# The normed operand of two stages made tile by tile in the last units of the stage in front, without a barrier at these two borders

## The chip, the cores and the metric

The kernel runs on one core of a Trainium2 chip. A core has a matrix engine (TensorE, "PE" in the profile, with its weight loads as "PEld"), a vector engine (VectorE, "DVE"), a scalar engine (ScalarE, "ACT"), GpSimd ("POOL") and a queue engine (SyncE, "SP"). Each runs its own instruction stream, and they wait for each other by semaphores. The metric is device time in microseconds (us) of the whole kernel, the median of several runs.

## What is computed

One step of a decoder layer on 1024 prompt tokens and 8 sample tokens (1032 columns in all), model width 1024, all in fp32:

```
x = x + 0.5 * swiglu(rmsnorm(x, g_ffn1), ffn1_gate, ffn1_up, ffn1_down)   # FFN 1
h = rmsnorm(x, g_mix);  proj = h @ w_in                                   # projections
...  # RWKV-7 branch y_a and S5 branch y_b from proj
merged = gates[..., :D_MODEL] * (y_a @ w_a_up) + gates[..., D_MODEL:] * (y_b @ w_b_up)
x = x + merged @ w_out                                                    # merge, out product
x = x + 0.5 * swiglu(rmsnorm(x, g_ffn2), ffn2_gate, ffn2_up, ffn2_down)   # FFN 2
# rmsnorm(x, g) = x * rsqrt(mean(x * x, axis=-1) + 1e-6) * g
```

## The kernel before

Activations lie transposed in SBUF: 128 channels on the partitions, 8 tiles (`DT`) of 1032 tokens. A **unit** is one 128-column stripe of a weight matrix times all tokens. The PE instructions of a unit are in `product`: for each of `kt` tiles of the contraction three groups of three matmuls of 344 columns (the fp32 operands are split into a high and a low part, high x high, high x low, low x high). So a unit with kt = 8 is 24 groups, and one of FFN 1's last down-projection units, with kt = 5, is 15. Two sets of three PSUM banks alternate between units.

Around each unit four things move. SP loads the weight stripe (`load_units`, L164) into one of two slots `wraw`; POOL splits it into `whi` (L176) and `wlo` (L179) as soon as the unit that used the slot two before is done; PE multiplies; DVE empties the banks and frees the set (`set_free`). The engines' order is that in which the code is written, engine by engine.

The norm is applied late. The operand of a normed product is x times g (`hhi` by ACT at L313, `hlo` by DVE at L321, a high and a low part), without the row factor; squares of x (ACT, L254) are summed over the 8 tiles (DVE, L261 and L264) into `ssum`, PE turns these into sums over channels (L274) inside the second unit of the stage, DVE takes the inverse root, PE spreads it to all partitions (L285), DVE copies it to `rstd` (L305), and whoever empties a bank multiplies by it. The first two units thus need only `hhi` and `hlo`; the third needs a free bank set and so `rstd`.

Each stage is a function that emits one program per engine. FFN 1 stands in a block of its own; projections and S5 stage share a block; the merge (products with `w_a`, then eight units with `w_out`, the out product) and FFN 2 have a block each. At the end of a block all engines meet at a barrier. So in front of the projections and of FFN 2 the order is: last unit on PE, last add of the product into x on DVE (L435, L2520), barrier, then ACT and DVE make `hhi` and `hlo` tile by tile from x (`h_act`, `h_dve`) and PE starts on the first tile (`h_products`). In the projections ACT first issues the DMA that saves x to DRAM (L812), and SP loads two constants (L785, L786) and the weights of the third and fourth unit; the weights of the first two are loaded and split ahead, in the stage in front (`Ahead`).

Of the kernel before, what the change touches and what calls it, by code (L numbers as in the profile page):

```python
# [12 lines left out]
P = 128  # L13
# [232 lines left out]

def squares_act(act, g, n, ready=None):

    for k in range(DT):
        if ready:  # L250
            ready(k)
        if k >= 2:
            act.wait_ge(g.ssum_step, DT * n + k - 1)
        act.activation(g.tmp[:, k % 2, :], g.x[:, k, :], ACT.Square).then_inc(g.sq_ready, 1)  # L254

def square_sum(v, g, n, k):

    v.wait_ge(g.sq_ready, DT * n + k + 1)
    if k == 0:  # L260
        v.tensor_copy(g.ssum[:, :], g.tmp[:, 0, :]).then_inc(g.ssum_step, 1)  # L261
    else:
        v.wait_ge(g.ssum_step, DT * n + k)
        v.tensor_tensor(g.ssum[:, :], g.ssum[:, :], g.tmp[:, k % 2, :], ALU.add)\  # L264
            .then_inc(g.ssum_step, 1)

def sums_pe(pe, g, n):

    pe.wait_ge(g.ssum_step, DT * (n + 1))  # L270
    if n:
        pe.wait_ge(g.rstd_ready, 3 * n)
    for j in range(NSS):
        last = pe.matmul(g.ps[0:SS, 6, j:j + 1], g.ssum[:, j * SS:(j + 1) * SS], g.seg[:, 2:3],  # L274
                         start=True, stop=True)
    last.then_inc(g.norm_ss, 1)
# [30 lines left out]

def h_act(act, g, gcol, n, ready=None):

    for k in range(DT):  # L310
        if ready:
            ready(k)
        act.activation(g.hhi[:, k, :], g.x[:, k, :], ACT.Copy, scale=g.vec[:, gcol + k:gcol + k + 1])\  # L313
           .then_inc(g.hhi_ready, 1)

def h_dve(v, g, gcol, n):

# [8 lines left out]
def h_products(pe, g, n, u, use, first_two, rest):  # L327
# [4 lines left out]
    if first_two:  # L332
        product(pe, g, 0, 0, u, DT, 0, use[0], 0, hi, lo, h_wait)
        product(pe, g, 0, 0, u + 1, DT, 1, use[1], 0, hi, lo, None, (6, lambda: sums_pe(pe, g, n)))
# [10 lines left out]
def ffn_block(nc, g, w_up, w_down, gcol, before=None, after=None, setup=None, ahead=None, loaded=False):  # L345
# [20 lines left out]
    with nc.Block() as block:  # L366
# [29 lines left out]
        def _(v):  # L396
            st = Steps(v, g.dve_s, g.dve_n)
            h_dve(v, g, gcol, n0)
# [5 lines left out]
            for size, k0, u, a, use, use1 in groups():  # L404
# [23 lines left out]
                if after and k0 + size == FT:  # L428
                    after["down"](v, ud)
                    continue  # L430
                with v.Fori(0, DT // 2) as i:
# [9 lines left out]
            g.dve_end = st.n  # L441

        @block.scalar
        def _(act):
            if before:
                before["scalar"](act)
            h_act(act, g, gcol, n0, before and before["x_ready"](act))
            squares_act(act, g, n0)
# [11 lines left out]
            if after:  # L460
                after["scalar"](act)
            if setup:
# [3 lines left out]
        def _(pe):  # L466
# [5 lines left out]
            for size, k0, u, a, use, use1 in groups():  # L472
                h_products(pe, g, n0, u, (use, use1), k0 == 0, size - (k0 == 0))
# [11 lines left out]
    g.a_tiles, g.norms, g.dve_n = a0 + FT, n0 + 1, g.dve_end  # L485
# [285 lines left out]
def proj_block(nc, g, w_in, shift, f_dram, x_dram, last_out, gp_dram, d_in, u_dram, us_dram, ahead, block):  # L771
# [10 lines left out]
    if block:  # L782
        @block.sync
        def _(sp):
            sp.dma_start(g.shift[:, :, :], shift).then_inc(g.sh_in, 16)  # L785
# [25 lines left out]
        def _(act):  # L811
            act.dma_start(x_dram, g.x[:, :, :]).then_inc(g.x_out, 16)  # L812
            h_act(act, g, V_GMIX, n0)
            squares_act(act, g, n0)
# [28 lines left out]
        def _(v):  # L843
            st = Steps(v, g.dve_s, g.dve_n)
            h_dve(v, g, V_GMIX, n0)
# [1594 lines left out]
def plan_merge(nc, g):  # L2440
    o = g.x_end
# [3 lines left out]
    g.mt, o = g.at("merge_t", o, [P, 2, TOK])  # L2445
    assert o <= g.u_off, (o, g.u_off)
    S = nc.alloc_semaphore
# [5 lines left out]
def merge_block(nc, g, w_a, w_out, gate_dram, wb_dram, x_dram, ahead):  # L2453
# [5 lines left out]
    t = g.mt  # L2459
# [4 lines left out]
    with nc.Block() as block:  # L2464
# [20 lines left out]
        def _(act):  # L2485
            for k in range(WT):
                act.activation(g.yahi[:, k, :], g.ya[:, k, :], ACT.Copy).then_inc(g.ya_hi_s, 1)
            for n in range(DT):
                act.wait_ge(g.m_ready, n + 1)
                act.activation(g.hhi[:, n, :], t[:, n % 2, :], ACT.Copy).then_inc(g.m_hi, 1)  # L2490
# [3 lines left out]
            for k in range(DT // 2, DT):  # L2494
                act.dma_start(g.x[:, k, :], x_dram[:, k, :]).then_inc(g.x_in[k], 16)

        @block.vector
        def _(v):
# [4 lines left out]
            for n in range(DT):  # L2503
# [11 lines left out]
                v.tensor_tensor(g.hlo[:, n, :], t[:, j, :], g.hhi[:, n, :].bitcast(F32),  # L2515
                                ALU.subtract).then_inc(g.m_split, 1)
            for n in range(DT):
                v.wait_ge(g.x_in[n], 32)
                v.wait_ge(g.unit_done, uo + n + 1 + WSLOTS)
                v.scalar_tensor_tensor(blocks(g.x[:, n, :]), acc(g, n % 2), 0.5, blocks(g.x[:, n, :]),  # L2520
                                       ALU.mult, ALU.add).then_inc(g.set_free[n % 2], 1)

        @block.tensor
        def _(pe):
# [3 lines left out]
            with pe.Fori(0, DT // 2) as i:  # L2528
                for j in range(2):
                    product(pe, g, i, 2, uo + j, DT, j, use_o[j], 1, part(g.hhi), part(g.hlo),  # L2530
# [7 lines left out]
def build(nc, a, o):  # L2538
# [36 lines left out]
    ffn_block(nc, g, a["ffn1_up"], a["ffn1_down"], V_G1,  # L2575
              before={"sync": first_loads, "scalar": first_x,
                      "x_ready": lambda act: lambda k: act.wait_ge(g.x_in[k], 16)},
              setup=s5_setup(g, s5_dram), ahead=ahead(a["w_mix"], DT, RT))
    consts, f_load = rwkv_early(g, f_dram, a["tabs"], a["lora_up"], a["g_up"], a["rw_sel"])
    with nc.Block() as block:  # L2580
        proj_block(nc, g, a["w_mix"], a["shift"], f_dram, x_dram, o["last"], s5_dram["in"], a["s5_d"], u_dram, us_dram,
# [5 lines left out]
    merge_block(nc, g, a["w_a"], a["w_out"], gate_dram, wb_dram, x_dram, ahead(a["ffn2_up"], DT))  # L2587

    n1 = g.norms + 1  # L2590
    ends = [n + 1 + FT + len(FFN_GROUPS) * DT // 2 for n in g.uses]
# [37 lines left out]
    ffn_block(nc, g, a["ffn2_up"], a["ffn2_down"], V_G2, loaded=True,  # L2629
# [108 lines left out]
```

## Time and profile before

| | us |
|---|---|
| median of 3 runs | 2828.43 (2824.94 to 2828.95) |
| profiled execution | 2827.97 |
| its span, first to last instruction | 2826.2 |
| PE busy | 2631.1 (93%) |
| DVE busy | 1143.4 (40%) |
| POOL busy | 891.9 (32%) |
| ACT busy | 429.9 (15%) |

Busy time is a sum over the span; it does not say who waits for whom. Matmuls are pipelined: a group of three is shown with a length of some 0.63 us, but the next one starts 0.47 us after it, so the pace is read from starts.
### The profile page before, as it was taken

The page shows a single profiled execution, that of the slowest core. Times are in us where ns is not written, and L with a number is a line of the kernel's source. Part 1 is how long each engine was busy: PE and PEld are TensorE (multiplying, and loading weights), DVE is VectorE, ACT ScalarE, POOL GpSimd, SP SyncE. Part 2 cuts the span into 40 slices and gives each one's busy share as a digit, 9 for nine tenths or more (in the row PEclk, how much of TensorE's full clock was granted, in tenths as well). Part 3 has the DMA queues.
Part 4 walks back from the last instruction along what each step waited for, and adds up shares of the span by engine and source line. Part 5 has one row for each costly group of instructions (what it writes and reads, how often), then busy time and mean ns, then how long its engine had stood idle before and what let it go on. Part 6 is the DMA issues. An engine that isn't in the chain of part 4 may idle for free. (4 is left out here: it accounts for less than half of the span.)

```text
span 2826.2 us, 47930 instructions
## 1 busy us (share of the span) xinstructions
PE 2631.1 (93%) x20824; PEld 2558.5 (91%) x20824; DVE 1143.4 (40%) x1637; ACT 429.9 (15%) x764; POOL 891.9 (32%) x445
## 2 busy tenths in 40 slices
PE   7999999999989989997899999569899999999997
PEld 7999999999989989996788887459899999999997
DVE  5743834713154555334444544253242122122224
ACT  3000100000020001122344443110111000000011
POOL 3444434444333432234100000005334444443432
PEclk9999999999999999998999989679999999999998
DMA  3112121111144242233310000024111111111111
GB/s 119 47 47 60 65 62 60 61 51 50 47 158 102 90 161 83 75 132 104 96 28 16 16 14 3 18 87 175 45 38 39 58 45 37 52 48 41 52 38 74
DMA packets 79684, 183.23 MB, mean 65 GB/s; under 512 B 11504, under 2 KB 34672, under 8 KB 78784
## 3 DMA queue, kind: packets, MB, share of 16 engines
q1 hardware_dynamic: 55456, 133.71, 15.4%
q10 hardware_dynamic: 24096, 47.59, 5.1%
q8 instruction: 103, 1.69, 0.3%
q14 instruction: 29, 0.24, 0.0%
HBM read 139.65 MB, written 40.44 MB: 64 GB/s over the span
## 5 line engine op out<-in xcount | busy, mean ns | idle before, releaser
L176 POOL TENSOR_TENSOR whi<-wraw,small 128x1024 fp32r<-128x1024 f32 (+3 forms) x214 | 363.3, 1697 | 1868.2 <-PE ps L210 1809.5
L210 PE MATMUL ps<-hhi,whi 128*128 128x344 f32 x3120 | 673.6, 325 | 54.5 <-POOL wlo L179 33.0
L210 PE MATMUL ps<-hlo,whi 128*128 128x344 f32 x3120 | 668.3, 323 | 0.0
L210 PE MATMUL ps<-hhi,wlo 128*128 128x344 f32 x3120 | 665.1, 322 | 0.0
L210 PEld LDWEIGHTS ps<-hhi,whi 128*128 128x128 f32 x3120 | 531.6, 191 | 57.3 <-issue 36.9
L210 PEld LDWEIGHTS ps<-hlo,whi 128*128 128x128 f32 x3120 | 534.3, 191 | 0.0
L210 PEld LDWEIGHTS ps<-hhi,wlo 128*128 128x128 f32 x3120 | 526.2, 190 | 0.0
L179 POOL TENSOR_TENSOR wlo<-wraw,whi 128x1024 fp32r<-128x1024 f32 (+3 forms) x214 | 516.0, 2411 | 16.8
L210 PE MATMUL ps<-ahi,whi 128*128 128x344 f32 x1056 | 223.8, 320 | 0.0
L210 PE MATMUL ps<-alo,whi 128*128 128x344 f32 x1056 | 223.5, 320 | 0.0
L210 PE MATMUL ps<-ahi,wlo 128*128 128x344 f32 x1056 | 223.0, 319 | 0.0
L435 DVE SCALAR_TENSOR_TENSOR x<-ps,x 128x1032 f32 x56 | 69.0, 1233 | 345.8 <-PE ps L210 345.8
L455 ACT ACTIVATE tmp<-tmp 128x1032 f32<-128x1032 f32 x44 | 47.0, 1068 | 888.1 <-DVE tmp L408 888.1
L411 DVE TENSOR_TENSOR tmp<-ps,rstd 128x1032 f32<-128x1032 f32 x44 | 54.2, 1232 | 304.5 <-PE ps L210 304.5
L210 PEld LDWEIGHTS ps<-ahi,whi 128*128 128x128 f32 x1056 | 177.0, 188 | 0.0
L210 PEld LDWEIGHTS ps<-alo,whi 128*128 128x128 f32 x1056 | 176.9, 188 | 0.0
L210 PEld LDWEIGHTS ps<-ahi,wlo 128*128 128x128 f32 x1056 | 176.8, 188 | 0.0
L408 DVE TENSOR_TENSOR tmp<-ps,rstd 128x1032 f32<-128x1032 f32 x44 | 54.2, 1233 | 178.0 <-PE ps L210 177.3
L419 DVE TENSOR_TENSOR alo<-tmp,ahi 128x1032 fp32r<-128x1032 f32 (+1 forms) x44 | 85.9, 1951 | 54.6 <-ACT ahi L457 54.6
L457 ACT ACTIVATE ahi<-tmp 128x1032 fp32r<-128x1032 f32 (+1 forms) x44 | 47.0, 1068 | 387.9 <-DVE tmp L416 387.9
L2048 PE MATMUL ps<-rw_x,rw_t 64*64 64x64 f32 x1280 | 86.5, 233 | 7.1 <-DVEq L1392 6.0
L2051 PE MATMUL ps<-rw_t,rw_x 64*64 64x64 f32 x1280 | 84.5, 230 | 0.0
(401 smaller groups left out, 2552.4 us busy)
## 6 DMA issues: line engine op xcount, KB each, us to landing
wraw<-ffn_up SPq DMA_DIRECT2D x88, 512.0 KB, 3.6
wraw<-ffn_down SPq DMA_DIRECT2D x32, 384.0 KB, 3.2
wraw<-ffn_down SPq DMA_DIRECT2D x32, 320.0 KB, 2.9
wraw<-w_mix SPq DMA_DIRECT2D x18, 512.0 KB, 3.6
gates<-gate_out ACTq DMA_DIRECT2D x16, 516.0 KB, 2.7
wraw<-w_gates SPq DMA_DIRECT2D x16, 512.0 KB, 3.7
f_mixed<-fmix ACTq DMA_DIRECT2D x14, 516.0 KB, 3.7
rw_f<-f_mixed SPq DMA_DIRECT2D x8, 896.0 KB, 5.7
```

What stands on the lines that cost most here:

```text
L176: pool.tensor_tensor(g.whi[:, s, 0:n], g.wraw[:, s, 0:n], g.zero.to_broadcast([P, n]), ALU.add).then_inc(g.w_hi, 1)
L179: pool.tensor_tensor(g.wlo[:, s, 0:n], g.wraw[:, s, 0:n], g.whi[:, s, 0:n].bitcast(F32), ALU.subtract).then_inc(g.w_split, 1)
L210: last = pe.matmul(g.ps[:, 3 * bank_set + b, 0:BLK], w[:, s, k * P:(k + 1) * P], x(k, b), start=(k == 0 and first), stop=(k == kt - 1 and ...
L408: v.tensor_tensor(blocks(g.tmp[:, 0, :]), acc(g, 0), blocks(g.rstd[:, :]), ALU.mult)\
L411: v.tensor_tensor(blocks(g.tmp[:, 1, :]), acc(g, 1), blocks(g.rstd[:, :]), ALU.mult)\
L419: v.tensor_tensor(g.alo[:, bass.ds(i, 1), :], g.tmp[:, 1:2, :], g.ahi[:, bass.ds(i, 1), :].bitcast(F32), ALU.subtract).then_inc(g.a_ready, 1)
L435: v.scalar_tensor_tensor(xt, acc(g, j), 0.5, xt, ALU.mult, ALU.add)\
L455: act.activation(g.tmp[:, 0, :], g.tmp[:, 0, :], ACT.Silu).then_inc(g.silu_done, 1)
L457: act.activation(g.ahi[:, bass.ds(i, 1), :], g.tmp[:, 1:2, :], ACT.Copy).then_inc(g.a_hi, 1)
L2048: pe.matmul(g.ps[r, 6 + n, p * N:(p + 1) * N], T[r, n, 1, p, :], g.X[r, j - 1, n, p, :], start=True, stop=True)
L2051: last = pe.matmul(g.ps[r, 6 + n, (4 + p) * N:(5 + p) * N], g.X[r, j - 1, n, p, :], T[r, n, 1, p, :], start=True, stop=True)
```

## The change

Three things. (1) FFN 1, projections and S5 stage now share one block, and merge and FFN 2 another: no barrier at these two borders. (2) The operand of the next normed stage is made in the last eight units of the stage in front: once DVE has added unit k into x, ACT makes `hhi` and the square of tile k, and DVE makes `hlo` and adds the square of tile k - 1 behind the add of unit k. Only the last tile's work comes behind the last add. (3) As `hhi` and `hlo` are now written while the out product still runs, the merge keeps its merged operand in tiles of its own (`mhi`, `mlo`, where FFN's `ahi` and `alo` lie), its inputs move into the space of `hhi` and `hlo`, and the squares and sums of the second border get tiles of their own (`tmp2`, `ssum2`). What the barrier had ordered for SP at the first border is now waited for by name.

```
+def h_hi(act, g, gcol, k):
+    act.activation(g.hhi[:, k, :], g.x[:, k, :], ACT.Copy, scale=g.vec[:, gcol + k:gcol + k + 1])\
+       .then_inc(g.hhi_ready, 1)
+def h_lo(v, g, gcol, n, k):
+    v.wait_ge(g.hhi_ready, DT * n + k + 1)
+    v.scalar_tensor_tensor(g.hlo[:, k, :], g.x[:, k, :], g.vec[:, gcol + k:gcol + k + 1],
+                           g.hhi[:, k, :].bitcast(F32), ALU.mult, ALU.subtract).then_inc(g.h_ready, 1)
...
 def ffn_block(...)
-    with nc.Block() as block:
+    if block:
...
         def _(v):
-            h_dve(v, g, gcol, n0)
+            if not normed:
+                h_dve(v, g, gcol, n0)
...
+                if gnext is not None and k0 + size == FT:
+                    for k in range(DT + 1):
+                        if k < DT:
+                            v.wait_ge(g.unit_done, ud + k + 1 + WSLOTS)
+                            v.scalar_tensor_tensor(blocks(g.x[:, k, :]), acc(g, k % 2), 0.5, blocks(g.x[:, k, :]),
+                                                   ALU.mult, ALU.add).then_inc(g.set_free[k % 2], 1)
+                        if k:
+                            h_lo(v, g, gnext, n0 + 1, k - 1)
+                            square_sum(v, g, n0 + 1, k - 1)
...
         def _(act):
+            if gnext is not None:
+                downs = [n + FT + (len(FFN_GROUPS) - 1) * DT // 2 for n in s0]
+                for k in range(DT):
+                    act.wait_ge(g.set_free[k % 2], downs[k % 2] + k // 2 + 2)
+                    h_hi(act, g, gnext, k)
+                    square_act(act, g, n0 + 1, k, g.tmp)
...
 def proj_block(...)
         def _(sp):
+            sp.wait_ge(g.unit_done, u0 + WSLOTS)
+            sp.wait_ge(g.su_ready, 12)
+            for n in range(3):
+                sp.wait_ge(g.su_out[n], 16 * 4)
             sp.dma_start(g.shift[:, :, :], shift).then_inc(g.sh_in, 16)
...
         def _(act):
             act.dma_start(x_dram, g.x[:, :, :]).then_inc(g.x_out, 16)
-            h_act(act, g, V_GMIX, n0)
-            squares_act(act, g, n0)
...
         def _(v):
-            h_dve(v, g, V_GMIX, n0)
...
 def merge_block(...)
         def _(act):
+            for k in range(DT):
+                act.wait_ge(g.set_free[k % 2], use_o[k % 2] + k // 2 + 2)
+                h_hi(act, g, V_G2, k)
+                square_act(act, g, n1, k, g.tmp2)
         def _(v):
-            for n in range(DT):
...
+            for n in range(DT + 1):
+                if n < DT:
+                    v.wait_ge(g.x_in[n], 32)
+                    v.wait_ge(g.unit_done, uo + n + 1 + WSLOTS)
+                    v.scalar_tensor_tensor(blocks(g.x[:, n, :]), acc(g, n % 2), 0.5, blocks(g.x[:, n, :]),
+                                           ALU.mult, ALU.add).then_inc(g.set_free[n % 2], 1)
+                if n:
+                    h_lo(v, g, V_G2, n1, n - 1)
+                    square_sum(v, g, n1, n - 1, g.ssum2, g.tmp2)
```

The order of ACT's program at the first border, before (from FFN 1's last turn, L457, to the save of u, L817):

```order
L457 ACTIVATE ahi<-tmp 128x1032 [waits a_full]
L366 UNCONDITIONAL_BRANCH [waits s5_part_out2,s5_part_out1,s5_part_out0]
L810 UNCONDITIONAL_BRANCH [waits barrier_Pool_Activation_PE_DVE_SP_release]
L812 DMA x_mid<-x 128x8256
L313 ACTIVATE hhi<-x,vec 128x1032 x8
L254 ACTIVATE tmp<-x 128x1032 x2
L254 ACTIVATE tmp<-x 128x1032 [waits square_sums] x6
L817 DMA u<-u_turned 128x1024 [waits u_ready]
```

and now (L314 is the old L313, L251 the old L254, L849 the old L812; the last three of the eight pairs stand here):

```order
L314 ACTIVATE hhi<-x,vec 128x1032 [waits set_free1]
L251 ACTIVATE tmp<-x 128x1032 [waits square_sums]
L314 ACTIVATE hhi<-x,vec 128x1032 [waits set_free0]
L251 ACTIVATE tmp<-x 128x1032 [waits square_sums]
L314 ACTIVATE hhi<-x,vec 128x1032 [waits set_free1]
L251 ACTIVATE tmp<-x 128x1032 [waits square_sums]
L847 UNCONDITIONAL_BRANCH [waits s5_part_out2,s5_part_out1,s5_part_out0]
L849 DMA x_mid<-x 128x8256
L852 DMA u<-u_turned 128x1024 [waits u_ready]
```

The sixteen instructions have moved in front of the stage's border, one pair behind each add into x, and the save of x has moved behind them.

On DVE at the second border, before (from the add of the out product's seventh unit into x to the first step of the inverse root):

```order
L2520 SCALAR_TENSOR_TENSOR x<-ps,x 128x1032 [waits unit_done,x_in6]
L2520 SCALAR_TENSOR_TENSOR x<-ps,x 128x1032 [waits unit_done,x_in7]
L2464 UNCONDITIONAL_BRANCH
L395 UNCONDITIONAL_BRANCH [waits barrier_Pool_Activation_PE_DVE_SP_release]
L321 SCALAR_TENSOR_TENSOR hlo<-x,vec,hhi 128x1032 [waits h_hi] x8
L261 COPY ssum<-tmp 128x1032 [waits squares_ready]
L264 TENSOR_TENSOR ssum<-ssum,tmp 128x1032 [waits square_sums,squares_ready] x7
L296 COPY small<-ps 86x12 [waits norm_sums]
```

and now (L2566 is the old L2520, L320 the old L321, L270 the old L264, L301 the old L296):

```order
L2566 SCALAR_TENSOR_TENSOR x<-ps,x 128x1032 [waits unit_done,x_in6]
L320 SCALAR_TENSOR_TENSOR hlo<-x,vec,hhi 128x1032 [waits h_hi]
L270 TENSOR_TENSOR ssum_150<-ssum_150,squares_149 128x1032 [waits square_sums,squares_ready]
L2566 SCALAR_TENSOR_TENSOR x<-ps,x 128x1032 [waits unit_done,x_in7]
L320 SCALAR_TENSOR_TENSOR hlo<-x,vec,hhi 128x1032 [waits h_hi]
L270 TENSOR_TENSOR ssum_150<-ssum_150,squares_149 128x1032 [waits square_sums,squares_ready]
L320 SCALAR_TENSOR_TENSOR hlo<-x,vec,hhi 128x1032 [waits h_hi]
L270 TENSOR_TENSOR ssum_150<-ssum_150,squares_149 128x1032 [waits square_sums,squares_ready]
L409 UNCONDITIONAL_BRANCH
L301 COPY small<-ps 86x12 [waits norm_sums]
```

Behind the last add there stand four of the sixteen instructions, where there were all sixteen and a barrier.

On PE at the first border, before (the last groups of FFN 1's last unit, then the projections' first):

```order
L210 MATMUL ps<-ahi,wlo 128x344 x3
L474 REGISTER_ALU
L474 COMPARE_AND_BRANCH
L366 UNCONDITIONAL_BRANCH
L906 UNCONDITIONAL_BRANCH [waits barrier_Pool_Activation_PE_DVE_SP_release]
L210 MATMUL ps<-hhi,whi 128x344 [waits h_ready,set_free0,weights_split]
```

and now:

```order
L210 MATMUL ps<-ahi,wlo 128x344 x3
L507 REGISTER_ALU
L507 COMPARE_AND_BRANCH
L940 UNCONDITIONAL_BRANCH
L210 MATMUL ps<-hhi,whi 128x344 [waits h_ready,set_free0,weights_split]
```

The wait for the barrier is gone; the three waits of the first matmul and one branch are left.

## Rows read from the trace of the kernel before

**Rows 1.** The page: busy time by engine, granted TensorE clock in 40 slices.
```profile
PE 2631.1 (93%) x20824; PEld 2558.5 (91%) x20824; DVE 1143.4 (40%) x1637; ACT 429.9 (15%) x764; POOL 891.9 (32%) x445
...
PEclk9999999999999999998999989679999999999998
```

**Rows 2.** What TensorE waited for: us in total, times, longest us.
```profile
PE ps L210 <- DVE hlo L321: 15.2, 2, 7.8
```

**Rows 3.** Timeline, first border: start us, us, engine, line, instruction, [idle before, releaser].
```profile
778.75 0.63 PE L210 MATMUL ps<-ahi,wlo 128*128 128x344 f32 x3
779.53 1.89 POOL L176 TENSOR_TENSOR whi<-wraw,small 128x1024 fp32r<-128x1024 f32 x1 [2.71 <-PE ps L210]
779.54 1.23 DVE L435 SCALAR_TENSOR_TENSOR x<-ps,x 128x1032 f32 x1 [5.87 <-PE ps L210]
781.50 2.34 POOL L179 TENSOR_TENSOR wlo<-wraw,whi 128x1024 fp32r<-128x1024 f32 x1
...
784.16 0.35 ACTq L812 DMA_DIRECT2D x_mid<-x  x1
...
784.55 4.29 ACT L313 ACTIVATE hhi<-x,vec 128x1032 fp32r<-128x1032 f32 x4 [58.27 <-PEq L366]
...
785.74 2.50 DVE L321 SCALAR_TENSOR_TENSOR hlo<-x,vec,hhi 128x1032 fp32r<-128x1032 f32 x2 [4.97 <-ACT hhi L313]
...
787.18 1.20 PE L210 MATMUL ps<-hhi,whi 128*128 128x344 f32 x3 [7.80 <-DVE hlo L321]
```

**Rows 4.** Timeline, second border.
```profile
2029.93 0.64 PE L210 MATMUL ps<-hhi,wlo 128*128 128x344 f32 x3
2030.67 1.23 DVE L2520 SCALAR_TENSOR_TENSOR x<-ps,x 128x1032 f32<-128x1032 f32 x1 [10.13 <-PE ps L210]
...
2035.35 4.29 ACT L313 ACTIVATE hhi<-x,vec 128x1032 fp32r<-128x1032 f32 x4 [95.54 <-PEq L2464]
...
2037.97 1.20 PE L210 MATMUL ps<-hhi,whi 128*128 128x344 f32 x3 [7.41 <-DVE hlo L321]
```

**Rows 5.** Windows behind each border (PEclk is the granted clock), then TensorE's timeline there.
```profile
787.00:793.00 6.00, 5.82 (x22) 5.85 (x23) 6.00 (x7) 6.00 (x7) 0.00 (x0) 0.54 0.86 369
...
2038.00:2042.00 4.00, 4.00 (x15) 4.00 (x16) 4.00 (x4) 4.00 (x5) 0.00 (x0) 0.53 0.46 176
...
792.48 0.64 PE L210 MATMUL ps<-hhi,whi 128*128 128x344 f32 x3
...
2042.13 0.63 PE L210 MATMUL ps<-hhi,wlo 128*128 128x344 f32 x3
```

**Rows 6.** Timeline, the last unit but one of FFN 1 on VectorE and GpSimd.
```profile
772.44 1.90 POOL L176 TENSOR_TENSOR whi<-wraw,small 128x1024 fp32r<-128x1024 f32 x1 [4.27 <-PE ps L210]
772.44 1.23 DVE L435 SCALAR_TENSOR_TENSOR x<-ps,x 128x1032 f32 x1 [5.86 <-PE ps L210]
...
774.42 2.40 POOL L179 TENSOR_TENSOR wlo<-wraw,whi 128x1024 fp32r<-128x1024 f32 x1
```

**Rows 7.** Lines L321 and L264 on VectorE: duration ns min/median/max.
```profile
L321 DVE SCALAR_TENSOR_TENSOR hlo<-x,vec,hhi x24: 1282/1285/3421, 8.4 to 2045.0; 128x1032 fp32r<-128x1032 f32 x24
...
L264 DVE TENSOR_TENSOR ssum<-ssum,tmp x28: 1223/1234/3254, 26.9 to 2800.5; 128x1032 f32<-128x1032 f32 x28
```

**Rows 8.** Windows behind the row sums, and TensorE's third product of the projections.
```profile
819.00:824.00 5.00, 4.29 (x17) 4.32 (x18) 2.53 (x6) 0.00 (x0) 0.38 (x2) 0.66 0.75 228
2059.00:2066.00 7.00, 6.99 (x48) 6.71 (x47) 2.92 (x14) 0.00 (x0) 0.00 (x0) 0.76 0.17 63
...
819.71 1.12 PE L210 MATMUL ps<-hhi,whi 128*128 128x344 f32 x3 [2.61 <-DVE u_turned L868]
```

**Rows 9.** TensorE at a border inside one block, projections to S5 stage.
```profile
1018.23 0.64 PE L210 MATMUL ps<-hhi,wlo 128*128 128x344 f32 x3
1018.71 0.63 PE L210 MATMUL ps<-hhi,whi 128*128 128x344 f32 x3
```

**Rows 10.** DMA issues from 783 to 812 us: KB each, median us to landing.
```profile
wraw<-w_mix SPq DMA_DIRECT2D x3, 512.0 KB, 13.4
```

More of the change, by code:

```diff
@@ L244, with square_act @@
 RB = 430
+def square_act(act, g, n, k, tmp):
+    if k >= 2:
+        act.wait_ge(g.ssum_step, DT * n + k - 1)
+    act.activation(tmp[:, k % 2, :], g.x[:, k, :], ACT.Square).then_inc(g.sq_ready, 1)
 def squares_act(act, g, n, ready=None):
@@ L273, in sums_pe @@
     for j in range(NSS):
-        last = pe.matmul(g.ps[0:SS, 6, j:j + 1], g.ssum[:, j * SS:(j + 1) * SS], g.seg[:, 2:3],
+        last = pe.matmul(g.ps[0:SS, 6, j:j + 1], (g.ssum if ssum is None else ssum)[:, j * SS:(j + 1) * SS], g.seg[:, 2:3],
                          start=True, stop=True)
@@ L341, in h_products, with ffn_block @@
             product(pe, g, i, 2, u + j, DT, j, use[j], 1, hi, lo)
-def ffn_block(nc, g, w_up, w_down, gcol, before=None, after=None, setup=None, ahead=None, loaded=False):
+def ffn_block(nc, g, w_up, w_down, gcol, before=None, after=None, setup=None, ahead=None, loaded=False, normed=False,
+              gnext=None, block=None):
     u0, s0, a0, n0 = g.units, list(g.uses), g.a_tiles, g.norms
@@ L446, in _ @@
                 before["scalar"](act)
-            h_act(act, g, gcol, n0, before and before["x_ready"](act))
-            squares_act(act, g, n0)
+            if not normed:
+                h_act(act, g, gcol, n0, before and before["x_ready"](act))
+                squares_act(act, g, n0)
             for size, k0, u, a, use, use1 in groups():
@@ L2458, in merge_block @@
     use_o = [n + DT // 2 for n in use_a]
-    t = g.mt
+    t, n1 = g.mt, g.norms
     def part(x):
         return lambda k, b: x[:, k, b * BLK:(b + 1) * BLK]
-    with nc.Block() as block:
+    if block:
         @block.sync
@@ L2489, in _ @@
                 act.wait_ge(g.m_ready, n + 1)
-                act.activation(g.hhi[:, n, :], t[:, n % 2, :], ACT.Copy).then_inc(g.m_hi, 1)
+                act.activation(g.mhi[:, n, :], t[:, n % 2, :], ACT.Copy).then_inc(g.m_hi, 1)
                 if n >= DT // 2:
@@ L2529, in _ @@
                 for j in range(2):
-                    product(pe, g, i, 2, uo + j, DT, j, use_o[j], 1, part(g.hhi), part(g.hlo),
+                    product(pe, g, i, 2, uo + j, DT, j, use_o[j], 1, part(g.mhi), part(g.mlo),
                             (g.m_split, lambda i, k: k + 1))
@@ L2628, in build @@
     g.y_ready = nc.alloc_semaphore("y_ready")
-    ffn_block(nc, g, a["ffn2_up"], a["ffn2_down"], V_G2, loaded=True,
-              after={"sync": final_out, "scalar": final_act, "down": final_down, "vector": final_dve,
-                     "tensor": final_pe})
+    with nc.Block() as block:
+        merge_block(nc, g, a["w_a"], a["w_out"], gate_dram, wb_dram, x_dram, ahead(a["ffn2_up"], DT), block)
+        ffn_block(nc, g, a["ffn2_up"], a["ffn2_down"], V_G2, loaded=True, normed=True, block=block,
+                  after={"sync": final_out, "scalar": final_act, "down": final_down, "vector": final_dve,
+                         "tensor": final_pe})
 OUTPUTS = {"y": (P, DT, TOK), "last": (P, RT, NB + 1), "wkv_prompt": (P, 4, N), "wkv_sample": (P, 4 * NB, N),
```

62 lines of the change are left out of this document (30 added, 32 removed).

## The prediction, made before the changed kernel had run

> **What bounds the kernel now.** I read the page first: TensorE is busy 93% of the span and its granted clock is near full in nearly every slice, every other engine under half [rows 1]. So time comes from two places only: stretches in which PE does nothing, and stretches in which it runs at the lower of its two clock levels. Next I read what PE waited for. One line stands out at the borders that the change touches: PE waited for `hlo` (DVE, L321) 15.2 us in total, twice, at most 7.8 us [rows 2]. Then the timeline at both places. At the first border, FFN 1 to projections, PE's last group starts at 778.75, the add into x runs from 779.54 to 780.77, then nothing computes until ACT issues the save of x at 784.16; the first `hhi` starts at 784.55, the first `hlo` at 785.74, PE's first group at 787.18 [rows 3]. The second border has the same steps: last group 2029.93, add 2030.67, `hhi` 2035.35, first group 2037.97 [rows 4]. Last the windows behind the gaps: the granted clock is 0.54 and 0.53 there [rows 5], which is the lower level (1.2 GHz) for most of the window, after PE had stood still.
>
> **The change part by part.** The pace first. Two consecutive adds of the last units lie 7.10 us apart (772.44 to 779.54, [rows 3, 6]); such a unit has 15 groups, so a group takes 0.473 us at full clock and a unit with 24 groups 11.36 us.
>
> *The gap goes.* At the first border the next group would start 0.47 behind the last one, at 779.22; it started at 787.18, so the gap costs 7.96 us [rows 3]. At the second: 2030.40 against 2037.97, 7.57 us [rows 4].
>
> *The low clock behind the gap goes.* First border: from 787.18 to the group at 792.48 there are 6 groups, 5.30 us where 6 x 0.473 = 2.84 would do: 2.46 us [rows 3, 5]. Second: from 2037.97 to 2042.13 there are 5 groups, 4.16 where 2.37 would do: 1.79 us [rows 4, 5]. With no gap PE goes on at the level at which it was.
>
> Sum: 7.96 + 7.57 + 2.46 + 1.79 = 19.8 us, if PE finds all three things that its first matmul waits for (an operand tile, a free bank set, a split weight) and the later tiles in time.
>
> *Is the operand there?* The last add is over at 780.77. Behind it DVE has `hlo` of tile 6, the sum of tile 6, `hlo` of tile 7, the sum of tile 7. Medians are 1.285 and 1.234 us [rows 7], so these end at 782.1, 783.3, 784.6 and 785.8. ACT needs 1.07 us for a `hhi` (four in 4.29, [rows 3]), and I count a square the same: `hhi` 7 is ready by 782.0. PE, started at 779.22 with 3 x 0.473 = 1.42 us a tile, wants tile 6 at 787.7 and tile 7 at 789.2: spare 5.7 and 4.6 us. The sum is wanted in the second unit, near 799. At the second border the offsets are the same within 0.2 us.
>
> *Is there room in the units before?* Per unit DVE now has 1.23 + 1.29 + 1.23 = 3.75 us of 7.10, and an add may come up to 5.8 us late before PE misses the bank set; ACT 2.14 of 7.10. In the out product a unit is 11.36 long. Hidden, at 0.
>
> *Weights.* The first unit's stripe is split from 772.44 to 776.82 [rows 6], the second's from 779.53 to 783.84 [rows 3], wanted at 779.2 and 790.6. The bank set of the first unit is freed by the add at 772.44. Nothing late.
>
> *SP's new waits.* Behind them on SP stand the two constants and the weight loads of the third and fourth unit. The last of them comes with FFN 1's last unit, about 779.5, earlier than the barrier's release did (784.1). The third unit's load then goes out near 780.3; even if it took the 13.4 us that such loads took beside the save of x [rows 10] it would be there at 793.7. GpSimd may split it only from 790.6 and takes 4.4 us, so 798.1 at the latest, and PE wants it when `rstd` is through, at 819.71 [rows 8] less the 10.4 us of this border, 809.3. Hidden.
>
> *The save of x* is moved behind the last square: hhi 7, square 7, so issued near 783.2 instead of 784.16, that is 7 us later against PE. It gates SP's load into x's place and, behind that, the fifth unit's weights, wanted more than 30 us later. Hidden; without that cover it would cost up to those 7 us.
>
> *What stays.* The row sums, the inverse root and the wait of the third unit for `rstd` hang on PE's own progress and shift with it. But the low level also appears there: 0.66 over 5 us at the first border and 0.76 over 7 us at the second [rows 8]. With the two levels at 1 and one half, the time lost in such a window is at most (1 - clock) x length: 1.7 us each. Whether the chip grants the low level there after a start without a gap no row shows. Bounds from these rows: each may vanish (-1.7) or come twice (+1.7). I take them as unchanged and keep +-3.4 for the range.
>
> The profiled execution took 2827.97; 2827.97 - 19.8 = 2808.2. The median of the runs is 0.46 above the profiled one, so I forecast 2808.6.
>
> A rule that speaks against this: the first matmul now stands right behind a branch into other code. The rows: at the border from projections to S5 stage, which lies inside one block and has such a branch too, PE's groups start at 1018.23 and 1018.71, 0.48 apart, no stall [rows 9]. The Trainium skill (Runtime: NRT & Kernel Launch, Instruction fetch mechanics) says that a taken branch whose target is outside the two pages held forces a fetch before execution goes on. By the trace the sum stays 19.8; by that rule something is taken off, and that is the first rival.
>
> **The rivals.**
>
> 1. *PE stalls at the branch, out of the loop of the last units into straight code.* For it: both borders leave a loop, the border of rows 9 does not. Against: rows 9, and no wait of PE in these stages but those named. Its price has no row; bounded from above by the time from the end of the add to the next instruction of any kind, 780.77 to 784.16, which holds barrier and branches: 3.4 us a border, and if the low clock comes back with it the 4.25 us above as well. 2808.6 + 6.8 = 2815.4, with the clock 2819.7.
>
> 2. *The last tiles come late.* DVE and GpSimd share work on SBUF while the second stripe is split; the longest `hlo` took 3.42 us and the longest sum 3.25 [rows 7]. At these, tile 7 is ready at 780.77 + 3.42 + 3.25 + 3.42 = 790.9, against 789.2: 1.7 us a border, 2812. Against: it needs three worst cases in a row, and the split ends by 784. The Trainium skill (GPSIMD Engine Reference, 1. Specifications) says that the two engines contend when a DVE instruction has two SBUF inputs; all the moved DVE instructions but two copies are such. That sentence gives no other time than this one.
>
> 3. *Slower than before: the splits outgrow the unit.* Mechanism: in FFN 1's last eight units each split now runs beside a `hlo` and a sum. GpSimd is done 4.38 us after the unit's end at its longest (772.44 to 776.82, [rows 6]), of 7.10, so 2.7 are spare. It decides from the point where a split is delayed by over 2.7 + 19.8 / 8 = 5.2 us. If DVE shut GpSimd out for all of a `hlo` and a sum at their longest, 6.67 us [rows 7], each of eight units lost 3.95 us: 2808.6 + 32 = 2840. Against: with median lengths the exclusion is 2.52 us, inside the spare time.
>
> 4. *The change doesn't do what it says:* something other than the barrier held PE as long. Time 2828. Against: all three waited-for things are accounted for above.
>
> **How the numbers follow.** The forecast 0.84, rival 1 0.06, rival 2 0.05, rival 3 0.02, rival 4 0.03. The forecast's own range is 2805 to 2812 (the two low-clock stretches). The runs of before spread over 4 us, and the range takes in rival 2 and the first form of rival 1: 2803.5 to 2815.5. About 0.2% (5.7 us) is what a measurement of this kernel can tell from no change; forecast and rivals 1 and 2 are all beyond it: faster 0.95, same 0.03, slower 0.02.
>
> **What would show it.** Right: between the last group with `ahi` and the first with `hhi`, and between the out product and FFN 2, PE's starts are 0.47 to 0.5 us apart and the clock there is 1.00; PE's wait for `hlo` is gone from the list; the last `hlo` starts 4 us before PE wants it; everything behind the first border lies 10.4 us earlier, behind the second 19.8. The splits of FFN 1's last eight units end within 7.1 us of their start. Wrong: a gap at the first `hhi` group put down to issue (rival 1); a wait for `hlo` at tile 6 or 7 (rival 2); waits for `wlo` in the last eight units (rival 3); more or longer half-clock windows behind the row sums.

## The result, and the profile after

Thirteen runs of each kernel gave a median of 2818.38 us now (2806.48 to 2823.42) against 2828.95 before (2824.94 to 2846.97). The ratio is 0.9946, with a 95% interval of 0.9927 to 0.9965: 0.54% faster, 15.3 us of 2829, where the prediction had 19.8 us. This ratio agrees with that of the means (2817.4 and 2832.7). The medians lie only 10.6 us apart, since the runs of before have a long upper end: five of the thirteen took over 2837 us. The interval leaves 1 out, so the kernel is faster, and the forecast's mechanism is what the trace shows; but the single profiled execution of now took 2823.37 us, only 4.6 less than before's 2827.97. So there are two questions: does each step stand in the trace, and where are the other 15 us of that execution?

The page of the kernel now, answering to [rows 1]. Every engine has as many instructions as before and is busy a little longer (GpSimd 901.1 for 891.9, VectorE 1164.1 for 1143.4). TensorE too is busy 11.1 us longer, 2642.2 for 2631.1; where, the table below shows:

```profile
PE 2642.2 (94%) x20824; PEld 2568.6 (91%) x20824; DVE 1164.1 (41%) x1637; ACT 431.1 (15%) x764; POOL 901.1 (32%) x445
...
PEclk9999999999999999997988899679999999999998
```

What TensorE waited for, the first rows, answering to [rows 2]. The row with `hlo` (15.2 us) is gone; the wait above it was there before (35.4):

```profile
PE ps L210 <- POOL wlo L179: 35.7, 6, 17.2
PE ps L2433 <- DVEq L1426: 13.6, 1, 13.6
PE ps L2395 <- ACT rw_lora L2298: 9.8, 1, 9.8
```

The timeline at the first border, answering to [rows 3] (L450 is the old L435, L849 the old L812):

```profile
771.70 1.23 DVE L450 SCALAR_TENSOR_TENSOR x<-ps,x 128x1032 f32<-128x1032 f32 x1 [2.14 <-PE ps L210]
...
778.12 0.63 PE L210 MATMUL ps<-ahi,wlo 128*128 128x344 f32 x3
...
778.59 0.64 PE L210 MATMUL ps<-hhi,whi 128*128 128x344 f32 x3
778.79 1.23 DVE L450 SCALAR_TENSOR_TENSOR x<-ps,x 128x1032 f32<-128x1032 f32 x1 [0.64 <-PE ps L210]
778.90 1.90 POOL L176 TENSOR_TENSOR whi<-wraw,small 128x1024 fp32r<-128x1024 f32 x1 [1.83 <-PE ps L210]
...
779.94 1.94 DVE L320 SCALAR_TENSOR_TENSOR hlo<-x,vec,hhi 128x1032 fp32r<-128x1032 f32 x1
...
780.32 0.34 ACTq L849 DMA_DIRECT2D x_mid<-x  x1
...
780.87 3.26 POOL L179 TENSOR_TENSOR wlo<-wraw,whi 128x1024 fp32r<-128x1024 f32 x1
...
781.12 1.06 ACT L251 ACTIVATE tmp<-x 128x1032 f32<-128x1032 f32 x1
...
781.81 3.42 DVE L270 TENSOR_TENSOR ssum<-ssum,tmp 128x1032 f32<-128x1032 f32 x1
...
785.15 1.28 DVE L320 SCALAR_TENSOR_TENSOR hlo<-x,vec,hhi 128x1032 fp32r<-128x1032 f32 x1
```

TensorE's last group with `ahi` starts at 778.12, its first with `hhi` at 778.59: 0.47 us, the steady pace, where there had been 8.43. The last sum but one holds VectorE until 785.23 (781.81 + 3.42), and the last `hlo` is there at 786.43. The second border, answering to [rows 4] (L2566 is the old L2520), looks the same, 2032.84 to 2033.31:

```profile
2032.84 0.64 PE L210 MATMUL ps<-merged_hi,wlo 128*128 128x344 f32 x3
2033.31 0.63 PE L210 MATMUL ps<-hhi,whi 128*128 128x344 f32 x3
2033.58 1.23 DVE L2566 SCALAR_TENSOR_TENSOR x<-ps,x 128x1032 f32<-128x1032 f32 x1 [4.99 <-PE ps L210]
...
2036.53 3.43 DVE L270 TENSOR_TENSOR ssum<-ssum,squares 128x1032 f32<-128x1032 f32 x1
```

The windows behind the borders, answering to [rows 5, 8] (the granted clock is the number in front of the last two): 1.00 where it had been 0.54 and 0.53. The low level is still there around the third product of each stage (0.72, and 0.81 over 14 us).

```profile
778.00:793.00 15.00, 15.00 (x97) 15.00 (x96) 8.96 (x8) 2.12 (x2) 7.83 (x4) 1.00 0.90 353
2033.00:2042.00 9.00, 9.00 (x59) 9.00 (x59) 8.42 (x5) 3.40 (x3) 5.16 (x2) 1.00 0.18 56
808.00:814.00 6.00, 5.38 (x24) 5.41 (x25) 2.44 (x6) 0.00 (x0) 0.31 (x2) 0.72 0.79 255
2053.00:2067.00 14.00, 12.05 (x84) 11.80 (x83) 7.73 (x20) 2.75 (x3) 4.24 (x2) 0.81 0.12 37
```

**The whole span cut at marks that both kernels have.** GpSimd begins a split (L176) 0.3 us after TensorE has begun the next unit, so its starts mark the ends of units to 0.1 us. The two marks around RWKV's chunks are TensorE's own: the ninth matmul on `rw_gup`, early in the chunks, and the first on `ya_hi`, with which the merge begins. At the first border, before (end of FFN 1's last unit; end of the third unit of the projections):

```profile
779.53 1.89 POOL L176 TENSOR_TENSOR whi<-wraw,small 128x1024 fp32r<-128x1024 f32 x1 [2.71 <-PE ps L210]
...
832.93 1.89 POOL L176 TENSOR_TENSOR whi<-wraw,small 128x1024 fp32r<-128x1024 f32 x1 [13.55 <-PE ps L210]
```

and now, from 778.90 (above) to:

```profile
821.83 1.90 POOL L176 TENSOR_TENSOR whi<-wraw,small 128x1024 fp32r<-128x1024 f32 x1 [13.52 <-PE ps L210]
```

Read so for two executions of each kernel (the second ones are the experiments e2 and e1 below):

| stretch, us | before | before again | now | now again |
|---|---|---|---|---|
| FFN 1, to the end of its last unit | 779.53 | 779.74 | 778.90 | 782.21 |
| border 1: three units of projections | 53.40 | 53.45 | 42.93 | 42.98 |
| projections, S5 stage and first chunks, to the `rw_gup` mark | 564.04 | 568.23 | 565.08 | 561.92 |
| RWKV's chunks from there, to the merge | 488.17 | 494.40 | 498.42 | 491.18 |
| merge, out product | 145.57 | 143.62 | 148.29 | 146.81 |
| border 2: three units of FFN 2 | 51.88 | 52.52 | 43.38 | 42.35 |
| the rest | 743.61 | 744.54 | 744.60 | 744.55 |
| span | 2826.2 | 2836.5 | 2821.6 | 2812.0 |

The two borders together are 19.0 us shorter in the first pair, 20.6 in the second. What hides this lies between the borders, in the third and fourth rows: together they take 1052.21 and 1062.63 us in the two executions of before, and 1063.50 and 1053.10 in the two of now. Each kernel was seen once in a short and once in a long form, over 10 us apart.

### The profile page after: what moved, and what is told of

Read it like the earlier page. It is cut to its first block and busy times, and to the rows that moved or that the text cites. A ratio compares the mean times of both kernels' runs of the same rounds, so it can differ in the third digit from the quotient of the medians.

```text
span 2821.6 us, 47886 instructions
## 1 busy us (share of the span) xinstructions
PE 2642.2 (94%) x20824; PEld 2568.6 (91%) x20824; DVE 1164.1 (41%) x1637; ACT 431.1 (15%) x764; POOL 901.1 (32%) x445
## 5 line engine op out<-in xcount | busy, mean ns | idle before, releaser
L176 POOL TENSOR_TENSOR whi<-wraw,small 128x1024 fp32r<-128x1024 f32 (+3 forms) x214 | 367.3, 1716 | 1852.8 <-PE ps L210 1794.2
L210 PE MATMUL ps<-hhi,whi 128*128 128x344 f32 x2928 | 629.9, 324 | 36.7 <-POOL wlo L179 30.4
L210 PE MATMUL ps<-hlo,whi 128*128 128x344 f32 x2928 | 625.7, 322 | 0.0
L210 PE MATMUL ps<-hhi,wlo 128*128 128x344 f32 x2928 | 622.6, 321 | 0.0
L210 PEld LDWEIGHTS ps<-hhi,whi 128*128 128x128 f32 x2928 | 497.0, 190 | 39.0 <-issue 18.4
L210 PEld LDWEIGHTS ps<-hlo,whi 128*128 128x128 f32 x2928 | 499.8, 191 | 0.0
L210 PEld LDWEIGHTS ps<-hhi,wlo 128*128 128x128 f32 x2928 | 492.3, 189 | 0.0
L460 DVE SCALAR_TENSOR_TENSOR x<-ps,x 128x1032 f32 x48 | 59.2, 1233 | 302.6 <-PE ps L210 302.6
```

What stands on the lines that cost most here:

```text
L176: pool.tensor_tensor(g.whi[:, s, 0:n], g.wraw[:, s, 0:n], g.zero.to_broadcast([P, n]), ALU.add).then_inc(g.w_hi, 1)
L210: last = pe.matmul(g.ps[:, 3 * bank_set + b, 0:BLK], w[:, s, k * P:(k + 1) * P], x(k, b), start=(k == 0 and first), stop=(k == kt - 1 and ...
L460: v.scalar_tensor_tensor(xt, acc(g, j), 0.5, xt, ALU.mult, ALU.add)\
```

## The experiments

**Is the missing time the kernel's or the execution's?** Both kernels were run again unaltered.

> The changed kernel, unaltered, once more. Theory A (the borders gave the 20 us, and what is missing is TensorE's granted clock in the RWKV stage, which falls differently in every execution): the stretch from the projections' third unit to the start of the merge, 1076.7 us in the changed kernel's trace and 1065.4 before, comes out anywhere between some 1060 and 1077, its length differing with the granted clock and not with the work; spans over the runs spread by 10 to 17 us in step with the clock. Rival B (the change makes the RWKV stage slower by 11 us each time): the stretch is again 1075 to 1078, with a clock as low as in the first trace. Time by A 2806 to 2823, mean near 2816; by B 2818 to 2824.

> The kernel before, unaltered, for a second trace of it. Theory A: the stretch from the projections' third unit to the merge differs from the 1065.4 us of the first trace, most likely longer, up to some 1085, since runs of this kernel reached 2847; the two borders read the same as in the first trace (gaps 7.8 and 7.4 us) within 0.2. Rival B: the stretch is 1065 +-2 and the time 2825 to 2830.

Measured: the kernel now has a median of 2813.05 (2804.85 to 2820.9, 6 runs) against 2832.24 (23 runs), ratio 0.9926, interval 0.9901 to 0.9951; its profiled execution a span of 2812.0. The kernel before, run once for its trace: 2838.32. Counted as the expectations do, from the projections' third unit to the merge, the stretch is 1066.3 us in the second trace of now (1076.7 in the first) and 1075.9 in the second of before (1065.4). That is what theory A said; rival B had 1075 to 1078 for the one and 1065 for the other. The second mark of the kernel before reads, in its second trace:

```profile
1401.42 1.16 PE L1972 MATMUL ps<-rw_lora,rw_gup 128*128 128x128 f32 x8 [0.83 <-ACT rw_e L1654]
```

The stretch of RWKV's chunks, in the order before, before again, now, now again, one window row from each trace (length first, TensorE's busy time next, the granted clock in front of the last two numbers):

```profile
1396.97:1885.14 488.17, 404.40 (x6412) 348.62 (x6413) 218.03 (x447) 175.85 (x453) 0.00 (x0) 0.85 0.06 17
```

```profile
1401.42:1895.82 494.40, 410.68 (x6413) 353.79 (x6413) 218.00 (x447) 175.97 (x453) 0.00 (x0) 0.83 0.06 17
```

```profile
1386.91:1885.33 498.42, 414.95 (x6413) 357.66 (x6413) 217.98 (x447) 176.21 (x453) 0.00 (x0) 0.83 0.06 16
```

```profile
1387.11:1878.29 491.18, 406.99 (x6413) 350.44 (x6413) 217.96 (x447) 175.96 (x453) 0.00 (x0) 0.84 0.06 17
```

VectorE and ScalarE are as busy in the long stretches as in the short ones (218.00 and 218.03; 175.97 and 175.85 in the kernel before). TensorE is busy 6.3 us longer in the one kernel and 8.0 in the other for the same instructions, which covers the 6.2 and 7.2 us by which the stretch grows, at a granted clock of 0.83 instead of 0.85 and 0.84. The other 3 to 4 us lie in the row above it in the table. The kernel before shows the long form as well as the short. So the stretch is long by the execution, not by the kernel, and the profiled execution of now happened to have the long form. In the traces of the five experiments below, third and fourth row together take 1049.0 to 1061.4 us. Over the 19 runs of the changed kernel span and mean clock move against each other (correlation -0.96; spans 2803.1 to 2821.6, clocks 0.954 to 0.948). Span times mean clock is therefore a quieter measure: medians of 2686.5 before (23 runs) and 2674.8 now (the 6 runs beside them), 11.7 apart, with a standard deviation of 0.9 to 2.3 between runs in all the comparisons here. The clock is on record to three decimals, so a single product is known to 1.4. It counts an idle or slow microsecond at the lower level as half, so it understates a gap; the experiments below are compared by it too, each against the runs of before beside it.

**The barrier or the place of the work?** Two kernels with one half of the change each. In e3 the barriers are gone, but the operand is made at the start of the next stage:

```
 # FFN 1: VectorE's plain loop of adds again; ScalarE waits for the last two adds
-                for k in range(DT):
-                    act.wait_ge(g.set_free[k % 2], downs[k % 2] + k // 2 + 2)
-                    h_hi(act, g, gnext, k)
-                    square_act(act, g, n0 + 1, k, g.tmp)
+                for j in range(2):
+                    act.wait_ge(g.set_free[j], downs[j] + DT // 2 + 1)
 # projections
+            h_act(act, g, V_GMIX, n0)
+            squares_act(act, g, n0)
...
+            h_dve(v, g, V_GMIX, n0)
 # merge: the same, behind all eight adds
```

> The barriers gone as in the change, but hhi, hlo, squares and sums made at the start of the next stage, behind the last add, as before. Theory C (the barrier waited for GpSimd, whose split ends 3.1 us behind the last add; hhi and hlo of the first tile then take 2.6 us more): PE's gap is add end to hhi 0.15 + 1.14 + hlo 1.29 + 0.15, so it starts 2.8 us behind the end of the add, a start-to-start gap of 4.4 to 4.7 us at each border in place of 8.0 and 7.6 and of 0.5 in the changed kernel; the low clock behind it stays at one border at least. Gain of 6.5 to 11 us against before. Rival D (most of the 8 us is the meeting of the engines and the branch): the gap falls to under 3.5 us. Time by C near 2820, by D near 2815, each +-7 for the clock elsewhere.

Measured: 2828.61 (10 runs), ratio 0.9989 (0.9973 to 1.0004), span times mean clock 1.2 below before: no change that these runs can tell. The timeline at the first border:

```profile
777.06 0.63 PE L210 MATMUL ps<-ahi,wlo 128*128 128x344 f32 x3
...
777.85 1.23 DVE L450 SCALAR_TENSOR_TENSOR x<-ps,x 128x1032 f32 x1 [5.87 <-PE ps L210]
...
779.72 8.48 ACT L314 ACTIVATE hhi<-x,vec 128x1032 fp32r<-128x1032 f32 x8 [55.13 <-DVE x L450]
779.81 2.35 POOL L179 TENSOR_TENSOR wlo<-wraw,whi 128x1024 fp32r<-128x1024 f32 x1
...
780.91 2.34 DVE L320 SCALAR_TENSOR_TENSOR hlo<-x,vec,hhi 128x1032 fp32r<-128x1032 f32 x1 [1.83 <-ACT hhi L314]
...
783.40 1.20 PE L210 MATMUL ps<-hhi,whi 128*128 128x344 f32 x3 [5.71 <-DVE hlo L320]
```

`hhi` starts 0.6 us behind the last add's end instead of 3.8 [rows 3], but TensorE gains only 2.09 us of its 7.80, not those 3.1: the first `hlo` starts while GpSimd splits (to 782.16) and takes 2.34 us, the longest in the stage, where 1.28 is its ordinary length. Neither theory hit: from group to group the gap is 6.34 us at both borders, where theory C had 4.4 to 4.7 and rival D under 3.5. C had the order of the steps right, `hhi` 0.5 us too early and the first `hlo` 1.05 us too short, and its gain of 6.5 to 11 us did not come: by the marks of the table the borders take 52.32 and 50.17 us, 2.8 less than before together.

In e4 the operand is made where the change makes it, and both barriers stand:

```
         ffn_block(nc, g, a["ffn1_up"], a["ffn1_down"], V_G1, ...)
+    with nc.Block() as block:
         proj_block(...)
...
         merge_block(...)
+    with nc.Block() as block:
         ffn_block(nc, g, a["ffn2_up"], a["ffn2_down"], V_G2, ...)
```

> The work made tile by tile in the last units as in the change, but both barriers kept. Theory C: the barrier is now released by VectorE, which has four instructions behind the last add and ends 6.3 us after PE's last unit (785.8 in place of GpSimd's 783.84), so PE starts some 6.8 to 7.3 us behind its last group, only 0.7 to 1.2 us less than before at each border, and the low clock stays: gain 1 to 3 us in all. Rival D (the barrier itself is cheap, what cost was making the first tile): the gap is under 5 us, gain over 6 us.

Measured: 2835.27 (10 runs), ratio 1.0008 (0.9986 to 1.0029), span times mean clock 1.8 above before; the expected gain of 1 to 3 us did not come. The gap is longer than before's, 9.24 us for 7.80, at the first border:

```profile
776.76 0.63 PE L210 MATMUL ps<-ahi,wlo 128*128 128x344 f32 x3
...
777.44 1.23 DVE L450 SCALAR_TENSOR_TENSOR x<-ps,x 128x1032 f32<-128x1032 f32 x1 [0.64 <-PE ps L210]
...
780.45 3.36 DVE L270 TENSOR_TENSOR ssum<-ssum,tmp 128x1032 f32<-128x1032 f32 x1
783.74 1.28 DVE L320 SCALAR_TENSOR_TENSOR hlo<-x,vec,hhi 128x1032 fp32r<-128x1032 f32 x1
784.94 1.22 DVE L270 TENSOR_TENSOR ssum<-ssum,tmp 128x1032 f32<-128x1032 f32 x1
786.46 0.38 ACTq L849 DMA_DIRECT2D x_mid<-x  x1
...
786.64 1.20 PE L210 MATMUL ps<-hhi,whi 128*128 128x344 f32 x3 [9.24 <-PEq L2625]
```

VectorE's tail behind the last add has become 7.5 us (777.44 + 1.23 = 778.67 to 786.16), and the first instruction behind the barrier comes 0.3 us after its end, TensorE's 0.48 us after. Theory C named VectorE as the one waited for, but summed its tail with the short durations (6.8 to 7.3 us from group to group, 9.88 measured): the sum took 3.36 us. That dates the old barrier too: in [rows 3] the last to finish was GpSimd with its split (781.50 + 2.34 = 783.84), and the first instruction behind the barrier came at 784.16, again 0.3 later. The meeting costs 0.3 us; the rest of the 3.4 us that the kernel before spent there was the wait for GpSimd's split. Neither half gives a gain in time that can be told from none: without the barrier alone the operand is late, and with the early operand alone the barrier waits for whoever is last, now VectorE.

**Are the two borders independent?** e5 has the change at the first border alone, e6 at the second alone:

```
 # e5: merge and FFN 2 as before (plain adds, a block each, no normed=True)
-                if n:
-                    h_lo(v, g, V_G2, n1, n - 1)
-                    square_sum(v, g, n1, n - 1, g.ssum2, g.tmp2)
+    with nc.Block() as block:
 # e6: FFN 1 without gnext, projections in a block of their own
-                  setup=s5_setup(g, s5_dram), gnext=V_GMIX, ahead=..., block=block)
+                  setup=s5_setup(g, s5_dram), ahead=..., block=block)
+    with nc.Block() as block:
```

> The change at the first border (FFN 1 to projections) alone; at the second the barrier stays and hhi, hlo, squares and sums are made behind it. Theory A (each border gives its gap and the low clock behind it, independently of the other): first border start to start 0.47, second 7.6; the third unit of the projections starts 10 to 11 us earlier than before, counted from PE's first group, and the whole is 10.4 us faster than before plus or minus what the RWKV stage's clock does (+-7): 2815 to 2830. Rival E (the gains overlap or the second is only there with the first): the second gap changes as well, or the first gives under 8.

> The change at the second border (merge to FFN 2) alone. Theory A: first border as before (8.0 us start to start), second 0.47; from the first out-product unit to FFN 2's third unit 9 to 10 us less than the 133.0 us of before; the whole 9.4 us faster plus or minus the RWKV stage's clock: 2816 to 2832. Rival E: under 8 us there.

Measured: e5 2825.1 (7 runs), ratio 0.9969 (0.9952 to 0.9986); e6 2826.62 (10 runs), ratio 0.997 (0.9957 to 0.9984). Each is faster, by 0.31% and 0.30%, and the sum, 0.61%, lies between the two measurements of the whole change (0.54 and 0.74%). By span times mean clock the halves give 5.6 and 6.3 of 2687.1, together 11.9, the whole 11.7. By the marks of the table the changed border takes 42.88 us in e5 and 42.35 in e6, the unchanged one 52.48 and 53.55, as in the traces of now and before. That is theory A at both borders. The untouched border keeps its gap: in e5 the second, in e6 the first.

```profile
2023.90 1.20 PE L210 MATMUL ps<-hhi,whi 128*128 128x344 f32 x3 [7.41 <-DVE hlo L320]
```

```profile
789.74 1.20 PE L210 MATMUL ps<-hhi,whi 128*128 128x344 f32 x3 [7.80 <-DVE hlo L320]
```

**What is late next?** The trace of now shows TensorE idle again 30 us behind each border: it has done two units, the row sums and the spreading of `rstd`, and waits for VectorE to free a bank set, and then runs at the lower level:

```profile
808.62 0.92 PE L210 MATMUL ps<-hhi,whi 128*128 128x344 f32 x3 [2.60 <-DVE u_turned L902]
809.35 1.06 PE L210 MATMUL ps<-hlo,whi 128*128 128x344 f32 x3
```

At these two borders the sums of squares are complete when the second unit begins, so the row sums need not wait for its seventh tile. e7 is the changed kernel with PE's row sums at the second tile and the spreading at the sixth (`product` takes several such insertions), in place of the seventh tile and the unit's end:

```
-        product(pe, g, 0, 0, u + 1, DT, 1, use[1], 0, hi, lo, None, (6, lambda: sums_pe(pe, g, n, ssum)))
-        rstd_pe(pe, g, n)
+        sums, spread = (6, lambda: sums_pe(pe, g, n, ssum)), (5, lambda: rstd_pe(pe, g, n))
+        product(pe, g, 0, 0, u + 1, DT, 1, use[1], 0, hi, lo, None,
+                ((1, sums[1]), (spread[0], spread[1])) if n else (sums,))
+        if not n:
+            rstd_pe(pe, g, n)
```

> The changed kernel, and on top of it the row sums on TensorE at the second tile of the second unit in place of the seventh, and the spreading of the inverse root at its sixth tile in place of behind the unit (projections and FFN 2; FFN 1 as it was). The sums' inputs lie ready since the last units of the stage in front. Theory F (the third unit's wait for rstd, 2.6 and 1.95 us, is only the latency of this chain, and the sums no longer have to wait): both waits vanish, and with them at most 1.7 us of low clock each: 4.5 to 8 us faster than the changed kernel, near 2810. Rival G (the spreading's wait for the inverse root, or VectorE's copies, now stall the second unit instead): a new wait of PE at L290 of 1 us or more, gain under 2 us.

Measured: 2809.49 (2793.9 to 2816.78, 6 runs), ratio to the kernel before 0.9901 (0.9875 to 0.9927); span times mean clock 2669.3, 17.8 below before, where the changed kernel in its own comparison was 11.7 below. The timeline, where the spreading now stands inside the second unit and TensorE goes on behind it:

```profile
794.46 1.93 PE L280 MATMUL ps<-seg,ssum 128*86 128x1 f32 x24
...
802.00 2.81 PE L291 MATMUL ps<-ident,small 86*128 86x86 f32 x24
...
804.60 0.72 PE L211 MATMUL ps<-hhi,whi 128*128 128x344 f32 x3
...
811.29 0.63 PE L211 MATMUL ps<-hhi,wlo 128*128 128x344 f32 x3
811.76 0.63 PE L211 MATMUL ps<-hhi,whi 128*128 128x344 f32 x3
```

By the marks of the table, border 1 is now 38.53 us (782.00 to 820.53) and border 2 38.56 (2027.42 to 2065.98), against 42.93 and 43.38 in the first trace of now (9.2 us less) and 42.98 and 42.35 in the second (8.2 less). TensorE waits at neither third unit any more, and in both borders' stretches the lower level is gone, which is theory F; it had 4.5 to 8 us. This version is faster than the kernel before. Against the changed kernel it was not timed side by side: its interval (0.9875 to 0.9927) and that of the first measurement of the change (0.9927 to 0.9965) only touch, while that of the second (0.9901 to 0.9951) overlaps with it, so that it is the faster of the two rests on the traces and on the 6.1 us between 17.8 and 11.7.

## Why the prediction came out as it did

*The sum.* The four terms belong together border by border. First border: 7.96 + 2.46 = 10.42 predicted, 53.40 - 42.93 = 10.47 found. Second: 7.57 + 1.79 = 9.36 predicted, 8.50 in the first pair (51.88 - 43.38) and 10.17 in the second (52.52 - 42.35). The gaps closed to 0.47 us, as said. The spread at the second border comes from the low level. Around the third unit the prediction held +-1.7 a border open: before, the third unit itself (from 2070.89) ran at full speed there; in the profiled execution of now the clock is 0.81 over 14 us (window row above), and in the second one 0.88 over the same 14 us:

```profile
2044.48:2058.48 14.00, 12.06 (x86) 11.81 (x85) 7.74 (x20) 2.77 (x3) 4.24 (x2) 0.88 0.13 37
```

Before differs as well (51.88 and 52.52): in its second execution the low level behind the gap lasted longer (a clock of 0.50 from 2046.71 to 2052.33, where the first has full speed again 4 us behind the gap).

*From the sum to the time.* Measured were 15.3 us (9.9 to 20.7 by the interval) and 21.0 (13.9 to 28.0); 19.8 lies in both. In absolute terms the median of 13 runs, 2818.4, is above the predicted range, and by the medians alone the gain is 10.6 us here and 19.2 in the second comparison. The range was set by the 4 us over which three runs of before had spread, while thirteen spread over 22, and the stretch between the borders alone moves an execution by 10. This is the one number behind the range that failed; scaled by the ratio (0.9946 of 2828.4 is 2813) the forecast held. That the first ratio came out 4.5 us short of the sum and the second 1.2 over it is within both intervals, and no run tells more.

*Is the operand there?* Right, but two durations in it were mis-sized, and that it held was partly luck. Predicted spare for tile 7: 4.6 us; found: ready at 786.43, wanted at 778.59 + 21 x 0.473 = 788.52, so 2.1 us. The step that was off is "Medians are 1.285 and 1.234 us": here `hlo` took 1.94 and the sum 3.42, since GpSimd splits at that time. Rival 2 said that lateness "needs three worst cases in a row". Two of its three operations do run long, and not by bad luck: at the second border the median of the seven sums is 3429 ns. What saved the forecast is that the third, the last `hlo`, comes when the split is over, and that its first operation could be held only for what was left of `whi` (0.86 us, 779.94 to 780.80).

```profile
L270 DVE TENSOR_TENSOR ssum<-ssum,squares x7: 1222/3429/3436, 1979.6 to 2041.1; 128x1032 f32<-128x1032 f32 x7
```

*Is there room in the units before?* Yes, with less to spare than 3.75 of 7.10 us suggested: of the 7.10 us between the last adds VectorE is idle for 0.64. Had the sum not been complete then, the add would have come later, up to the 5.8 us it may. GpSimd's split ends 5.23 us after its start (778.90 to 784.13) in place of 4.4, of 7.1. Rival 3 named the right mechanism and the wrong size: the splits lost 0.9 us each, 2.7 were spare.

*Rival 1.* Fallen: 0.47 us between the groups at both borders, no issue time at the branch out of the loop.

*Rival 4*, that something other than the barrier held TensorE. Fallen: the gap is gone, and so is the wait for `hlo`. But the barrier alone was not it either: without it, with the operand made behind it (e3), 5.71 of the 7.80 us stay.

*SP's waits, the weights, the save of x.* No new wait for `wlo` (35.7 us against 35.4), none for weights. The save of x was predicted behind the last square, near 783.2; it went out at 780.32, while that square was still to run. It needs x alone, and ScalarE's queue issued it ahead of the engine's work.

*The barrier.* The prediction took the 3.4 us from add to release as one piece, "barrier and branches". e4 shows that 0.3 of it is the meeting. That did not touch the sum, as all of it went.

## What to carry to other kernels

A gap at a stage border is worth its length plus what TensorE loses at its lower level behind it, and both can be read from the starts of groups; here that sum was right to 0.1 us at one border and to 0.9 at the other. Taking the barrier away and making the operand early gave no measurable time singly: work that is to be hidden has to stand in front of the last unit, and nothing may make TensorE wait for the slowest engine there. When VectorE work with two SBUF inputs is moved into a stage in which GpSimd is busy, count it at its longest duration in the trace, not its median; and before a 0.5% effect is read from two profiles, run both kernels twice.

## What the hardware showed that I had not expected

VectorE instructions with two inputs in SBUF and GpSimd's splits exclude each other, instruction by instruction. In the timeline of now at the first border, `hlo` starts at 779.94 and ends at 781.88, 1.08 us after the end of `whi` (780.80); the sum starts at 781.81 and ends at 785.23, 1.10 after the end of `wlo` (784.13). So nearly the whole of their ordinary length, 1.28 and 1.23 us, lies behind the split. And `wlo` takes 3.26 us instead of the 2.40 of [rows 6], as it waits for `hlo` to end. The add into x, with one input in PSUM and one in SBUF, takes 1.23 us beside a split as without. The kernel before had a striking case already: an instruction on 8 columns took 2.37 us, and ended at 860.92, just after the split (860.90).

```profile
857.63 3.27 POOL L179 TENSOR_TENSOR wlo<-wraw,whi 128x1024 fp32r<-128x1024 f32 x1
858.55 2.37 DVE L886 TENSOR_TENSOR fmix<-shift,fraw 128x8 f32<-128x8 f32 x1
```

The Trainium skill (SBUF — State Buffer, SBUF: two separate sides) describes this: a pair of ports to SBUF is shared by the two engines, whichever starts first has it for its whole instruction, and a VectorE instruction with two SBUF inputs needs it. The trace agrees, to the 0.1 to 0.2 us by which an instruction ends sooner behind the other than its ordinary length; what the prediction lacked was to count with it from the kernel before's own rows.

The other is the granted clock of RWKV's stretch, whose products are short and have gaps between them: 0.83 to 0.85 from one execution to the next with the same instructions, worth 6 to 7 us of 490, and over 10 with the stretch in front of it. The first 100 us of a run vary in the same way: in the two executions of the changed kernel their clock is 0.97 and 0.93, and FFN 1 ends at 778.90 and at 782.21. Why one execution gets less than another no run here tells.
